# Output stage of a hybrid decoder layer: tiles in another order, transposes inside later products, feed-forward products at the stage's end

## The reference, cut to what matters

```python
x = x + rmsnorm(merged @ w_o, g_post_mix)
h = rmsnorm(x, g_pre_ffn)
up = h @ w_up                       # 1024 -> 8192
acc = causal depthwise conv of width 3 over tokens, plus bias
a, b = split(acc)
x = x + rmsnorm((gelu(a) * b) @ w_down, g_post_ffn)
```

## Time and profile before

| | |
|---|---|
| median of 3 runs | 2200.75 us (2200.16 to 2202.24) |
| the profiled execution, its own time | 2201.84 us |
| its span in the trace | 2200.2 us |
| granted clock of PE, mean over the span | 0.973 of full speed |
| PE busy | 2056.8 us (93%) |
| DVE, ACT, POOL busy | 1265.9, 711.6, 547.4 us |

### The profile page before, as it was taken

One profiled execution on the slowest core, in us unless ns is written; L12 is line 12 of the kernel. 1 busy time (PEld: TensorE's weight loads), 2 busy tenths in 40 slices (PEclk: granted clock), 3 DMA queues, 4 the chain that ended last, 5 costly groups with the idle time before them and its releaser, 6 DMA issues.

```text
span 2200.2 us, 33028 instructions
## 1 busy us (share of the span) xinstructions
PE 2056.8 (93%) x12955; PEld 1905.2 (87%) x12955; DVE 1265.9 (58%) x2056; ACT 711.6 (32%) x1045; POOL 547.4 (25%) x428
## 2 busy tenths in 40 slices
PE   5999999999889879798899999999999999999997
PEld 5969889889756549776799999999999999999997
DVE  5789899899276634335344455344544445444555
ACT  4343333323366421134232223222232222322233
POOL 0323334112243231210122222222222222222220
PEclk9999999999899789899899999999999999999998
DMA  5202222323210253332111111111111111111123
GB/s 149 63 29 87 78 86 80 95 85 96 74 65 2 88 147 120 115 125 77 39 49 49 47 51 39 49 45 43 49 49 46 42 48 49 44 44 49 49 87 113
DMA packets 176802, 150.59 MB, mean 68 GB/s; under 512 B 29594, under 2 KB 150842, under 8 KB 176514
## 3 DMA queue, kind: packets, MB, share of 16 engines
q1 hardware_dynamic: 175370, 144.20, 21.4%
q0 software_dynamic: 1280, 4.20, 0.6%
HBM read 119.50 MB, written 27.95 MB: 67 GB/s over the span
## 4 chain that ended last, share of the span: by engine, by line
PE 44%; DVE 4%; issue 2%; DMA 0%; DVEq 0%; SPq 0%
PE ps L58 44%; DVE f_acc L2493 1%; DVE g_fT L2525 1%; DVE f_acc L2502 1%; DVE f_acc L2494 1%; DMA f_x<-d_x 0%; PE ps L2637 0%; DVE f_x L2578 0%; PE ps L2629 0%; DVE f_acc L2533 0%; DVE g_fT L2523 0%; DVE f_acc L2509 0%; DVEq L2520 0%; DVEq L2493 0%; PE ps L2620 0%
## 5 line engine op out<-in xcount | busy, mean ns | idle before, releaser
L58 PE MATMUL ps<-g_xT_h,f_wh 128*128 128x344 f32 x1536 | 492.9, 321 | 7.2 <-issue 5.0
L58 PE MATMUL ps<-g_xT_l,f_wh 128*128 128x344 f32 x1536 | 491.4, 320 | 0.0
L58 PE MATMUL ps<-g_xT_h,f_wl 128*128 128x344 f32 x1536 | 491.2, 320 | 0.0
L2367 POOL TENSOR_TENSOR f_wl<-f_wst,f_wh 128x1024 fp32r<-128x1024 f32 x94 | 245.9, 2616 | 383.1 <-ACT f_wh L2413 383.1
L58 PEld LDWEIGHTS ps<-g_xT_h,f_wh 128*128 128x128 f32 x1536 | 289.1, 188 | 9.1 <-issue 7.3
L58 PEld LDWEIGHTS ps<-g_xT_h,f_wl 128*128 128x128 f32 x1536 | 289.3, 188 | 0.0
L58 PEld LDWEIGHTS ps<-g_xT_l,f_wh 128*128 128x128 f32 x1536 | 289.2, 188 | 0.0
L1092 PE MATMUL ps<-g_hT_h,j_wh 128*128 128x344 f32 (+1 forms) x840 | 285.4, 340 | 0.0
L1092 PE MATMUL ps<-g_hT_l,j_wh 128*128 128x344 f32 (+1 forms) x840 | 268.7, 320 | 0.0
L1092 PE MATMUL ps<-g_hT_h,j_wl 128*128 128x344 f32 (+1 forms) x840 | 268.7, 320 | 0.0
L58 PE MATMUL ps<-f_gh,f_wh 128*128 128x344 f32 x768 | 248.9, 324 | 7.5 <-DVE g_fT L2525 6.9
(11 more groups left out here) (428 smaller groups left out, 3355.2 us busy)
## 6 DMA issues: line engine op xcount, KB each, us to landing
f_wst<-in_w_up SPq DMA_DIRECT2D x64, 512.0 KB, 4.0
j_wst<-in_w_in SPq DMA_DIRECT2D x34, 512.0 KB, 4.6
f_wst<-in_w_down SPq DMA_DIRECT2D x32, 512.0 KB, 3.6
d_gates<-j_ring SPq DMA_DIRECT2D x16, 516.0 KB, 3.0
m_gt<-d_gates SPq DMA_DIRECT2D x16, 516.0 KB, 4.8
a_k<-in_cache_k SPq DMA_DIRECT2D x16, 256.0 KB, 2.8
o_wst<-in_w_o SPq DMA_DIRECT2D x8, 512.0 KB, 3.8
o_x<-in_x_prompt SPq DMA_DIRECT2D x8, 512.0 KB, 4.8
```

Of the source, the lines that this page charges most:

```text
L58: mm = pe.matmul(ps[0:m, 3 * slot + c, 0:CH], w[:, k, 0:m], x[:, k, c * CH:(c + 1) * CH], start=(first and k == 0 and n == 0), stop=(last ...
L2367: pool.tensor_tensor(wl[:, s, :], wst[:, s, :], wh[:, s, :].bitcast(F32), ALU.subtract).then_inc(w_lo, 1)
```

## The change

It has six edits.

1. The sample tile is handled fourth (`order`, `tiles`, `SAM`); the other tiles keep their order.
2. In the lead, a slice's products with the high part of the weights need `w_hi` alone and come first; those with the low part come behind them, after `w_lo`.
3. Turns 1 to 5 stand inside the products of later tiles (`during`: after a given block k of a given tile).
4. `high(6)` comes behind the first square of tile 8, and `low(6)` ahead of the second norm of tile 8.
5. Behind the last product PE does two of the three thirds of the first two up-projection units (`first_third`), in turn with the turns 6 to 8. `ups` does only the last third of them.
6. The third and fourth weight tiles are loaded at the end of the output stage (`load_next`); at the start of the feed-forward part ACT makes the high part of the third ahead of the first evacuation, and POOL's low parts stand one place earlier in its order.

```diff
-def project(pe, ps, slot, wh, wl, xh, xl, kt, m=P, first=True, last=True):
-    for c in range(3):
+def project(pe, ps, slot, wh, wl, xh, xl, kt, m=P, first=True, last=True, cs=range(3)):
+    for c in cs:
...
-        LEAD, YB = 3, 6
+        LEAD, YB, SAM = 3, 6, 3
+        order = [0, 1, 2, NT, 3, 4, 5, 6, 7]
+        tiles = [TILES[j] for j in order]
...
             store(7)
+            for j in range(2):
+                g.ffn.load_next(sp, g, j)
             store(8)
...
                 act.wait_ge(z_done, i + 1)
+                square(i, 0)
                 if i == 8:
                     high(6)
-                square(i, 0)
...
                 dve.wait_ge(x2_done, i + 1)
+                if i == 8:
+                    low(6)
                 norm(i, 1)
...
-                if i >= 2:
+                if 2 <= i < 8:
                     low(i - 2)
...
-            def products(i, k):
-                t0, n = TILES[i]
-                for q, (x_, w) in enumerate(((g.xT_h, wh), (g.xT_h, wl), (g.xT_l, wh))):
+            PARTS = ((g.xT_h, wh), (g.xT_l, wh), (g.xT_h, wl))
+            def products(i, k, parts):
+                t0, n = tiles[i]
+                for q in parts:
+                    x_, w = PARTS[q]
...
             for k in range(KD):
+                pe.wait_ge(w_hi, k + 1)
+                for i in range(LEAD):
+                    products(i, k, (0, 1))
                 pe.wait_ge(w_lo, k + 1)
                 for i in range(LEAD):
-                    mm = products(i, k)
+                    mm = products(i, k, (2,))
                     if k == KD - 1:
                         mm.then_inc(done, 1)
+            during = {(5, 2): 1, (6, 1): 2, (7, 0): 3, (8, 0): 4, (8, 5): 5}
             for i in range(LEAD, 9):
                 pe.wait_ge(z_done, i - 2)
                 for k in range(KD):
-                    mm = products(i, k)
+                    mm = products(i, k, range(3))
+                    if (i, k) in during:
+                        turn(during[i, k])
                 mm.then_inc(done, 1)
-                for j in {3: (0,), 4: (1,), 5: (2,), 6: (3, 4), 7: (5,), 8: (6, 7, 8)}[i]:
-                    turn(j)
+                if i == LEAD:
+                    turn(0)
+            g.ffn.first_third(pe, g, 0, 0)
+            turn(6)
+            g.ffn.first_third(pe, g, 1, 0)
+            turn(7)
+            g.ffn.first_third(pe, g, 0, 1)
+            turn(8)
+            pe.wait_ge(z_done, 9)
+            g.ffn.first_third(pe, g, 1, 1)
...
+    def load_next(self, sp, g, j):
+        up_v = g.w_up.rearrange("(k p) n -> p k n", p=P)
+        sp.wait_ge(self.w_lo, j + 1)
+        sp.dma_start(self.wst[:, j, :].rearrange("p (k n) -> p k n", k=KD),
+                     up_v[:, :, j * FF + P:j * FF + 2 * P]).then_inc(self.w_in[j], 16)
+
+    def first_third(self, pe, g, j, c):
+        w3, l3 = (w[:, j, :].rearrange("p (k n) -> p k n", k=KD) for w in (self.wh, self.wl))
+        pe.wait_ge(self.w_lo, j + 1)
+        return project(pe, g.ps, j, w3, l3, g.xT_h, g.xT_l, KD, cs=(c,))
...
-            for q in (2, 3):
-                load(q, q % 2, 0, q)
...
             for q in range(4):
-                if q:
-                    low(q + 1, (q + 1) % 2)
+                if q < 3:
+                    low(q + 2, q % 2)
                 keep_cols(0, q)
...
                 for q in range(4):
+                    early = isinstance(it, int) and it == 0 and q == 0
+                    if early:
+                        high(it, q + 2)
                     evacuate(it, q)
+                    if early:
+                        continue
...
-                project(pe, ps, r, w3, l3, g.xT_h, g.xT_l, KD).then_inc(up_done, 1)
+                part = (2,) if isinstance(it, int) and it == 0 and q < 2 else range(3)
+                project(pe, ps, r, w3, l3, g.xT_h, g.xT_l, KD, cs=part).then_inc(up_done, 1)
```

More of the change, by code:

```diff
@@ L2090, in rows @@
         def rows(i):
-            return TILES[i][1]
+            return tiles[i][1]
         @block.sync
@@ L2104, in store @@
             def store(i):
-                t0, n = TILES[i]
+                t0, n = tiles[i]
                 sp.wait_ge(x2_done, i + 1)
                 sp.dma_start(g.d_x2[t0:t0 + n, :], z[0:n, i % 2, :]).then_inc(x2_out[i % 2], 16)
-            for i, (t0, n) in enumerate(TILES):
+            for i, (t0, n) in enumerate(tiles):
                 if i >= 2:
                     store(i - 2)
-                src = g.x_prompt.rearrange("b t d -> (b t) d")[t0:t0 + n, :] if i < NT else \
+                src = g.x_prompt.rearrange("b t d -> (b t) d")[t0:t0 + n, :] if i != SAM else \
                     g.x_sample.rearrange("b t d -> (b t) d")
```

## The result

The changed kernel takes 2174.86 us (median of 4 runs, 2172.15 to 2178.31), before 2200.72 us (4 runs, 2200.16 to 2202.24): a ratio of 0.9881, 95% interval 0.9868 to 0.9895, 25.9 us faster. The forecast was 2173.3 us, range 2170 to 2179 (its own narrower range 2170.5 to 2176).

What follows compares the result with a forecast made beforehand. PE was taken to bound the kernel, its idle and half-clock time in the output stage being the prize. Lead 2.4, middle 8.0 and tail 17.2 us, less 0.1 rounding, gave 27.5 off 2200.75: 2173.3 us, range 2170 to 2179.

Steps and rivals of the forecast that it cites:

- The bound: Whole kernel: PE, busy 93% of the span, sets the end; time saved in the output stage shortens the kernel equally.
- The stretch: From the output stage's first product to the third up-projection unit's first matmul: forecast from 921.2 to 1055.9.
- Lead: Output stage's first 144 matmuls: PE starts on ACT's high part instead of POOL's low part, 2.4 us earlier.
- Middle: Six tiles and six turns behind the lead: 72.0 us, 72.4 with the copy wait, against 80.39; 8.0 us gained.
- Tail: From the last output-stage product to the third up-projection unit: 25.9 us against 43.08, 17.2 gained.
- The sum: Over the whole change: 2.4 + 8.0 + 17.2 = 27.6 us, less 0.1 for rounding, 27.5 us.
- that is edit 4's worth: At turn 7: in the old order low(6) would end at 1041.5 and the turn would wait 3 us.
- (a): Middle: ACT and DVE's chain comes late and turns wait inside products; 2181 us, or 2177 for half; chance 0.12.
- (e): Six tiles: turns wait for low parts behind later norms; slower, 2209 us at 18 us a tile; chance 0.02.
- (c): Tail: early thirds not hidden, holding turns 7 and 8 up; 15.1 us go back, 2188 us; chance 0.03.
- (d): Feed-forward part: it gives the gained time back to some other wait, so no change; chance 0.02.
- (b): Granted clock falls at turns or between thirds; 1.7 us for each of five inner turns, 2182 us; chance 0.05.

Runs made afterwards that it cites:

- the runs on the thirds: Changed kernel without up-projection thirds in the output stage: 2189.73 us; with only the first third of the first two units there: 2181.99 us.
- the three traces: Profiles of the unedited changed kernel: the first and two repeats; median times 2174.86, 2173.44 and 2175.59 us.
- one pair of thirds: Changed kernel with only the first third of the first two up-projection units in the output stage, two thirds left to the feed-forward part: 2181.99 us.
- half of edit 4 undone: Changed kernel with low(6) again behind the second norm of the last tile and its xn, high(6) still behind the first square: 2180.18 us.
- turns behind: Changed kernel with turns 1 to 5 behind whole tiles again, the sample tile still fourth: 2181.89 us.
- the early slice: Changed kernel plus the first slice of w_o loaded at the end of the phase before, into its own buffer: 2170.20 us.

## Why the prediction was right

**The bound.** It rested on one reading: PE sets the end, and where it is idle or slow in the output stage is the whole prize. The stretch is 134.66 us against 134.7 forecast (1055.9 − 921.2); of the 25.2 us that it lost 20.3 are idle time; the other 4.9 are busy time, at a granted clock of 0.98 instead of 0.92.

**Lead.** Forecast 2.4 us. From ACT's first high part to the first product it was 923.58 − 920.05 = 3.53 us, and is 924.40 − 923.29 = 1.11 after: 2.42. With the edit undone the path to the third unit is 2.1 to 2.5 us longer. The wait for the first copy was 0.18 us, not 0.4.

**Middle.** Forecast 72.0 us for six tiles and six turns, measured 1033.11 − 961.01 = 72.10. No turn waits, the clock stays at 1.00; the place of the turns is worth 6.8 to 7.2 us of the 8.0, by the traces of the changed kernel.

**Tail.** Forecast 25.9 us, measured 1059.06 − 1033.11 = 25.95. The margins were 2.0, 0.8 and 1.3 us against 2.0, 0.65 and 1.4 forecast. The block's end left PE idle for 0.30 us; with the drain of the last matmul it cost 1051.32 − 1046.19 − 0.79 − 3.86 = 0.48, against 0.55. A third behind a turn took 1046.19 − 1041.54 − 0.79 = 3.86 us and not 3.78. The last two thirds and the wait for POOL took 7.74 us against 7.85. These errors are small, and they cancel. The thirds are worth 14.9 us, the order at the hand-over 2.4 to 2.9. Such worths do not add up to the gain, since each is measured with the other edits in place: ACT's half of edit 4, for one, counts because a third now stands ahead of turn 6.

**The sum.** From ACT's first high part to the third unit, 1083.44 − 920.05 = 163.39 us before; after 135.77, 135.36 and 135.37: 27.6 to 28.0 us against 27.6. The medians differ by 25.9. The rest is not in the stage: in the profiled execution ACT's first high part came 3.2 us later than before, and the time behind the third unit was 2176.6 − 1059.06 = 1117.54 us, 0.8 more than before (2200.2 − 1083.44 = 1116.76). The forecast of the median missed by 1.6 us, which is less than the medians of the changed kernel differ among themselves (2173.44 to 2175.59).

**The step that failed** is a price inside the tail: "that is edit 4's worth", 3 us. I had followed `low(6)` on DVE and not `high(6)` on ACT. The DVE half alone is worth 3.2 to 3.6 us (a wait of 3.06), as priced; both are worth 9.7 to 10.1, because an ACT that waits for turn 6 holds the last tile's squares, and all behind them. The sum did not need this price, since the edit was there.

**Rivals.** (a) and (e) fall with the waits table; (c) with the runs on the thirds; (d) with the time behind the third unit: 1117.54, 1116.79 and 1118.39 us in the three traces against 1116.76 before, so at most 1.6 us of the 27.6 came back. (b), the clock, did not come: nine turns, clock 1.00. The Trainium skill ("TensorE: Matmul & The Clock Gate", Part 4: PE-mode transpose) says that the full clock doesn't engage for transposes, which don't count as PE being busy in the same way. Among products the trace shows no effect of that. In the run with one pair of thirds the clock was at half behind a turn between two waits, which fits; but no run has these two waits without the turn, so this doesn't show that rule.

## What to carry to other kernels

Where an engine that sets the end waits for a chain on other engines, find work of the next stage whose inputs are ready and put it between the waits in pieces no longer than the chain needs: here four thirds of 3.8 us filled three waits and the gap at the block's end (pieces of another length were not tried). Moving work ahead of a step delays everything that waits for that step, so look on each engine at what is queued behind the wait: without the new order on ACT and DVE ten of the fifteen us that the thirds bring would have been lost. And count the stretch between two landmarks when runs differ by more than the edit is worth.

## What was not expected

A block's end leaves PE idle for only 0.30 us when PE is the last to arrive; in all the runs where the four thirds stood at the end it was the same figure.

Which waits cost the clock: one of 3.06 us did not (half of edit 4 undone), one of 3.77 us did (turns behind), and 2.46 and 2.64 us with only a turn between them did too (one pair of thirds). So the longest single wait does not tell whether the clock falls.

The code ahead of the stage is the same in all kernels but the one with the early slice, and yet ACT's first high part of `w_o` started between 917.75 and 923.29 us in the three traces of the changed kernel. That spread of 5.5 us is larger than the effects of the lead, the hand-over, the DVE half of edit 4 and the early slice. Only distances between landmarks in one trace could tell those apart: the stretch, the path from ACT's first high part, and for the early slice PE's idle time ahead of its first product.
